# Output projections that begin with the upper features of three tiles, in the ring's banks

## What is computed

```
# first block, per layer
x = x + 0.5 * swiglu(rmsnorm(x), ...)
x = x + mixer(rmsnorm(x))          # layer 0: HGRN2, layer 1: forgetting attention (FoX)
x = x + 0.5 * swiglu(rmsnorm(x), ...)
# inside a mixer: o is (256, 1024), 8 or 16 heads side by side, times a gate
return o @ w_out                    # w_out is 1024 x 1024
# second block, per layer
mix = nsa_mixer(...)  or  mla_mixer(...)            # 12 heads of 64
xa = memory_cross_attention(xq, mk, mv)             # 4 heads of 64
y = concatenate([mix, xa], -1) @ w_out[i]
x = layer_norm(ALPHA * x + y);  x = layer_norm(ALPHA * x + hier_moe(x))
```

## Time and profile before

| | |
|---|---|
| runs of the kernel | 2225.61, 2226.37, 2236.63 us, median 2226.37 |
| profiled execution | 2233.53 us, of which its span is 2231.7 us |
| mean granted clock of TensorE | 0.978 |
| PE busy | 2108.8 us (94%), 14195 matmuls |
| DVE busy | 1483.2 us (66%) |
| ACT busy | 1157.1 us (52%) |
| POOL busy | 26.1 us (1%) |
| HBM read | 416.7 MB, 187 GB/s over the span |

### The profile page before, as it was taken

How to read it: one execution, slowest core, us unless ns; L and a number is a source line. 1 busy time by engine, 2 the same in 40 slices (tenths; PEclk the granted TensorE clock), 3 DMA queues, 4 the chain that set the end, 5 groups by cost and what they waited for, 6 DMA issues and landing times. The chain is left out here.

```text
span 2231.7 us, 36800 instructions
## 1 busy us (share of the span) xinstructions
PE 2108.8 (94%) x14195; PEld 1892.5 (85%) x14195; DVE 1483.2 (66%) x2248; ACT 1157.1 (52%) x1655; POOL 26.1 (1%) x34
## 2 busy tenths in 40 slices
PE   7999999999999999889999988999999989999997
PEld 6999897999999978779998977787778758778876
DVE  5665675665666644476564456789888466888896
ACT  4343533534444335464433336678776455777774
POOL 1000000000000020000000000000000000000000
PEclk9999999999999999999999979999999999999999
DMA  8555222654445523334454521599996514799991
GB/s 278 191 196 177 95 82 90 216 179 169 170 170 175 197 80 128 138 114 170 169 186 143 148 73 58 180 328 334 342 317 212 217 38 170 244 318 325 318 358 56
DMA packets 312310, 421.09 MB, mean 189 GB/s; under 512 B 7844, under 2 KB 266304, under 8 KB 312096
## 3 DMA queue, kind: packets, MB, share of 16 engines
q1 hardware_dynamic: 308864, 415.93, 54.5%
q10 hardware_dynamic: 2816, 2.38, 0.5%
q0 software_dynamic: 544, 1.62, 0.2%
HBM read 416.70 MB, written 1.05 MB: 187 GB/s over the span
## 5 line engine op out<-in xcount | busy, mean ns | idle before, releaser
L2816 DVE TENSOR_TENSOR w_lo<-weight_ring,w_hi 128x1024 fp32r<-128x1024 f32 x384 | 449.3, 1220 | 35.9 <-ACT w_hi L2665 31.2
L569 PE MATMUL banks<-x_hi,w_hi 128*128 128x256 f32 x1408 | 401.0, 285 | 8.5 <-DVE w_lo L522 7.7
L570 PE MATMUL banks<-x_lo,w_hi 128*128 128x256 f32 x1408 | 399.3, 284 | 0.0
L571 PE MATMUL banks<-x_hi,w_lo 128*128 128x256 f32 x1408 | 399.3, 284 | 0.0
L2665 ACT ACTIVATE w_hi<-weight_ring 128x1024 fp32r<-128x1024 f32 x384 | 382.3, 1053 | 21.4 <-PE banks L2552 21.3
L515 ACT ACTIVATE w_hi<-weight_ring 128x1024 fp32r<-128x1024 f32 x88 | 93.0, 1057 | 418.5 <-PE banks L571 418.3
L887 DVE TENSOR_TENSOR pieces<-weight_ring,pieces 128x512 fp32r<-128x512 f32 (+2 forms) x245 | 166.3, 689 | 193.8 <-ACT pieces L876 192.3
L876 ACT ACTIVATE pieces<-weight_ring 128x512 fp32r<-128x512 f32 (+2 forms) x245 | 150.9, 627 | 251.3 <-PE banks L823 244.5
L569 PEld LDWEIGHTS banks<-x_hi,w_hi 128*128 128x128 f32 x1408 | 271.2, 193 | 10.8 <-DVE w_lo L522 8.6
L570 PEld LDWEIGHTS banks<-x_lo,w_hi 128*128 128x128 f32 x1408 | 271.3, 193 | 0.1
L571 PEld LDWEIGHTS banks<-x_hi,w_lo 128*128 128x128 f32 x1408 | 271.2, 193 | 0.0
(11 more groups left out here) (367 smaller groups left out, 3907.3 us busy)
## 6 DMA issues: line engine op xcount, KB each, us to landing
weight_ring<-in_ffn_w_in SPq DMA_DIRECT2D x88, 1024.0 KB, 7.5
weight_ring<-in_moe_w_gate SPq DMA_DIRECT2D x64, 1024.0 KB, 6.6
weight_ring<-in_moe_w_up SPq DMA_DIRECT2D x64, 1024.0 KB, 9.2
weight_ring<-in_moe_w_down SPq DMA_DIRECT2D x64, 1024.0 KB, 11.1
weight_ring<-in_ffn_w_out SPq DMA_DIRECT2D x44, 1024.0 KB, 9.6
weight_ring<-in_hg_w_in SPq DMA_DIRECT2D x12, 1024.0 KB, 8.2
weight_ring<-in_fox_w_in SPq DMA_DIRECT2D x12, 1024.0 KB, 8.5
weight_ring<-in_nsa_w_in SPq DMA_DIRECT2D x10, 1024.0 KB, 7.8
```

The source lines that it names most:

```text
L569: pe.matmul(out, w_hi, m_hi, start=start, stop=False, skip_group_check=True)
L570: pe.matmul(out, w_hi, m_lo, start=False, stop=False, skip_group_check=True)
L571: return pe.matmul(out, w_lo, m_hi, start=False, stop=stop, skip_group_check=True)
L2816: dve.tensor_tensor(self.piece(s, p, self.w_lo), self.piece(s, p), self.piece(s, p, self.w_hi.bitcast(F32)), ALU.subtract).then_inc(sem[ki ...
```

## The change

The order of the pieces of w_out becomes (tile 0, upper half), (1, upper), (2, upper), (0, lower), (1, lower), (2, lower), and from tile 3 on tile by tile as before. The results go to four banks of the ring, two tiles each, in place of banks 0 to 3; DVE releases each bank once its residual is written. Low and high parts of `cat` are made by helpers of their own (`act_cat_hi`, `dve_cat_lo`), and in the attention stages three of each, and the first three pieces, move into the last steps of the loops. A quarter is collected ahead of the score of its step. The last pair is always copied by ACT. `pr` no longer uses `wide[:, 0]`, which now takes high parts during the attention; two of its pairs lie in a region that only Ffn and Moe use otherwise. In Hgrn2 the pieces and the first two low parts come between the second and the third quarter.

```diff
--- before.py
+++ after.py
...
+        with ExitStack() as split:
+            split.enter_context(nc.sbuf_tensor("before_units", [P, ARENA + 4 * KD * T], F32))
+            self.more_units = split.enter_context(nc.sbuf_tensor("more_units", [P, 2, 2, 2 * T], F32))
...
         self.act_pieces(act, self.in_pieces + PIECES)
-        for c in range(4):
-            act.wait_ge(self.cat_ready, c + 1)
-            act.activation(k.half[0][:, 2 * c:2 * c + 2], k.cat[:, 2 * c:2 * c + 2], ACT.Copy).then_inc(k.xs_hi, 1)
+        for c in range(self.act_cat, 4):
+            self.act_cat_hi(act, c)
         self.act_pieces(act, "out7")
 
+    def act_cat_hi(self, act, c):
+
+        k = self.k
+        act.wait_ge(self.cat_ready, c + 1)
+        act.activation(k.half[0][:, 2 * c:2 * c + 2], k.cat[:, 2 * c:2 * c + 2], ACT.Copy).then_inc(k.xs_hi, 1)
+        self.act_cat = c + 1
+
+    def dve_cat_lo(self, dve, c):
+
+        k, cs = self.k, slice(2 * c, 2 * c + 2)
+        dve.wait_ge(k.xs_hi, self.hi0 + 4 + c + 1)
+        dve.tensor_tensor(k.half[1][:, cs], k.cat[:, cs], k.half[0][:, cs].bitcast(F32), ALU.subtract).then_inc(k.xs_lo, 1)
+        self.dve_cat = c + 1
+
     def release(self, eng, fill):
 
...
     def plan_out(self, name, w_out):
         k = self.k
-        self.w_out, self.out_fills = w_out, [k.ring.plan(1), k.ring.plan(1)]
+        self.w_out, self.out_fills, self.out_name = w_out, [k.ring.plan(1), k.ring.plan(1)], name
+        self.act_cat = self.dve_cat = 0
...
+        k = self.k
         self.in_pieces = len(self.piece_list)
-        for n in range(KD):
+        self.out_order = [(n, half) for half in range(2) for n in range(PIECES)] + [(n, half) for n in range(PIECES, KD) for half in range(2)]
+        self.out_piece = {}
+        for n, half in self.out_order:
             fill = self.out_fills[n // 4]
-            w = self.k.ring.slot(fill)[:, 0:4096].rearrange("p (k n) -> p k n", k=KD)
-            self.jobs[f"out{n}"] = self.plan_pieces(fill, w, slice((n % 4) * P, (n % 4 + 1) * P), 4)
+            w = k.ring.slot(fill)[:, 0:4096].rearrange("p (k n) -> p k n", k=KD)
+            self.out_piece[n, half] = k.n_pieces
+            self.piece_list.append((k.n_pieces, fill, w[:, 4 * half:4 * half + 4, (n % 4) * P:(n % 4 + 1) * P]))
+            k.n_pieces += 1
             self.job_end[f"out{n}"] = len(self.piece_list)
+
+    def plan_out_banks(self):
+        for c in range(4):
+            self.k.banks.plan_by(f"{self.out_name}_o{c}", self.k.piece_used, PIECES + self.out_piece[2 * c + 1, 1] + 1)
...
     def pe_out(self, pe):
-        k = self.k
-        for n in range(KD):
-            self.pe_tile(pe, k.acc[:, n], self.jobs[f"out{n}"], P, (k.half[0], k.half[1]), None if n else self.cat_split)
+        k, b = self.k, self.k.banks
+        for n, half in self.out_order:
+            name, m = f"{self.out_name}_o{n // 2}", self.out_piece[n, half]
+            if n % 2 == 0 and half == 0:
+                b.claim(pe, name)
+            out = b.at(name)[:, n % 2 * T:(n % 2 + 1) * T]
+            hi, lo = self.piece_parts(m, 4, P)
+            pe.wait_ge(k.piece_lo, m + 1)
+            for j in range(4):
+                kk = 4 * half + j
+                if n == 0 and kk % 2 == 0:
+                    pe.wait_ge(k.xs_lo, 4 * self.cat_split + kk // 2 + 1)
+                last = self.pe_three(pe, out, (hi[:, j], lo[:, j]), (k.half[0][:, kk], k.half[1][:, kk]), n % 2 == 0 and kk == 0, kk == KD - 1)
+            last.then_inc(k.piece_used, 1)
 
     def dve_out(self, dve, scale=1.0):
 
         k = self.k
         self.dve_pieces(dve, self.in_pieces + PIECES)
+        for c in range(self.dve_cat, 4):
+            self.dve_cat_lo(dve, c)
         for c in range(4):
-            cs = slice(2 * c, 2 * c + 2)
-            dve.wait_ge(k.xs_hi, self.hi0 + 4 + c + 1)
-            dve.tensor_tensor(k.half[1][:, cs], k.cat[:, cs], k.half[0][:, cs].bitcast(F32), ALU.subtract).then_inc(k.xs_lo, 1)
-        for c in range(4):
-            cs = slice(2 * c, 2 * c + 2)
+            cs, name = slice(2 * c, 2 * c + 2), f"{self.out_name}_o{c}"
             self.dve_pieces(dve, f"out{min(2 * c + 3, KD - 1)}")
-            dve.wait_ge(k.piece_used, PIECES + self.jobs[f"out{2 * c + 1}"][-1] + 1)
-            dve.scalar_tensor_tensor(out=k.x[:, cs], in0=k.x[:, cs], scalar=scale, in1=k.acc[:, cs],
+            src = k.banks.wait(dve, name).rearrange("p (k t) -> p k t", k=2)
+            dve.scalar_tensor_tensor(out=k.x[:, cs], in0=k.x[:, cs], scalar=scale, in1=src,
                                      op0=ALU.mult, op1=ALU.add).then_inc(k.x_ready, 1)
+            for done in ([], [0], [1], [2, 3])[c]:
+                dve.wait_ge(k.x_ready, 4 * self.turn + done + 1)
+                k.banks.release(dve, f"{self.out_name}_o{done}")
...
         k.banks.plan("hg_n", *[f"hg_r{n}" for n in range(4)])
+        self.plan_out_banks()
...
             dve.tensor_tensor(k.cat[:, hs], self.og[:, hs], src, ALU.mult).then_inc(self.cat_ready, 1)
             dve.wait_ge(self.cat_ready, n + 1)
             b.release(dve, f"hg_r{n}")
+            if n == 1:
+                self.dve_pieces(dve, self.in_pieces + PIECES)
+                self.dve_cat_lo(dve, 0)
+                self.dve_cat_lo(dve, 1)
         self.dve_out(dve)
...
-        self.pr = [part(t)[:, r] for t in (at, flat(k.wide[:, 0])) for r in range(2)]
+        self.pr = [part(at)[:, r] for r in range(2)] + [k.more_units[:, r] for r in range(2)]
...
             k.banks.plan(f"{name}_s{i}_0", f"{name}_s{i}_1")
+        self.plan_out_banks()
...
     def copied_by_dve(self, j):
-        return j % 4 == 3
+        return j % 4 == 3 and j < len(self.pairs) - 1
...
             if 0 <= j < n and not self.copied_by_dve(j):
                 out, src = self.copy_in(act, j)
                 act.activation(out, src, ACT.Copy).then_inc(k.att_copied, 1)
+            if step >= n - 1:
+                self.act_drain(act, step - n + 1)
             if step < n:
                 c = (self.u0 + step) % 4
                 for half in range(2):
@@ -1371,8 +1417,12 @@
                         e = self.pr[step % self.DEEP][:, half, at:at + w]
                         act.activation(e, e, ACT.Exp, scale=-1.0, bias=k.att_cols[:, 0, c, t, half:half + 1],
                                        accum_out=k.att_cols[:, 1, c, t, half:half + 1]).then_inc(k.att_exp, 1)
-        act.wait_ge(k.att_turned, self.u0 + n)
-        self.act_pieces(act, self.in_pieces + PIECES)
+    def act_drain(self, act, at):
+
+        if at != 2:
+            self.act_cat_hi(act, (0, 1, None, 2)[at])
+        if at:
+            self.act_pieces(act, self.in_pieces + at)
 
     def dve_units(self, dve):
...
-            if step < n:
-                self.dve_score(dve, step)
-            if 1 <= step < n + 1:
-                self.dve_weight(dve, step - 1)
             if q < 4 and step - self.VALUE_LAG - 1 >= self.quarter_end[q]:
                 self.dve_quarter(dve, q)
                 q += 1
-        self.dve_pieces(dve, self.in_pieces + PIECES)
+            if step < n:
+                self.dve_score(dve, step)
+            else:
+                self.dve_cat_lo(dve, step - n)
+            if 1 <= step < n + 1:
+                self.dve_weight(dve, step - 1)
+            if step >= n:
+                self.dve_pieces(dve, self.in_pieces + step - n + 1)
         while q < 4:
             self.dve_quarter(dve, q)
             q += 1
```

## The result

The changed kernel took 2217.66 us (median of 14 runs, 2212.14 to 2223.54) beside 2231.98 us for the kernel before (14 runs, 2225.45 to 2236.63): a ratio of 0.9941, 95% interval 0.9930 to 0.9952, so 13.1 us less. The forecast was 13.0 us less, 2213.4 beside the 2226.37 of that time. A second measurement, at the end of the study, gave 2218.94 us and 0.9959 (0.9945 to 0.9973), 9 us less; the two intervals overlap from 0.9945 to 0.9952, 11 to 12 us less. The profiled execution took 2213.9 us, its span is 2212.0 (before: 2231.7).

What follows compares the result with a forecast made beforehand. PE was busy 2108.81 of 2231.70 us, so time could be won only where it idles or runs at the lower clock. Terms: 6.9 - 0.2 + 4.3 + 2.0 + 0.4 - 0.4 = 13.0 us less, 2213.4; range 2206 to 2222.

Steps and rivals of the forecast that it cites:

- Start of the projection: In FoX, NSA and MLA, PE's waits before the out projection go: 6.88 us gained, less 0.2 for FoX.
- Cover: In the FoX, NSA and MLA projections, the fourth piece is ready 0.6 us before PE wants it: no cost.
- Rival C: The projection runs dry at its fourth piece in three stages: only 4 to 8 us gained; chance 0.08.
- Clock behind the starts: In FoX, NSA and MLA, the first projection matmuls no longer run at the low clock: 4.3 us gained.
- Rival B: The clock falls all the same in the attention stages: only 8.7 us gained, 2217.7; chance 0.19.
- HGRN2's start: In HGRN2, the first low part comes earlier and PE starts the projection 2.03 us earlier.
- HGRN2's clock: In HGRN2's projection, the clock's return gains 0.4 us, taken between 0.8 worse and 1.2 better.
- The added waits: DVE's wait on its own last residual before releasing a bank delays both Ffn stages: 0.4 us lost.
- Quarters ahead of scores: In the attentions, collecting a quarter before a score gains nothing, within 0.3 us either way per attention.
- step 1: In FoX, NSA and MLA, the out projection starts without PE's wait: 6.88 us gained, less 0.2 for FoX.
- Rival E: Kernel slower: new half-clock stretches, up to 13.5 us each, two needed to be over 0.5% slower, 2240; chance 0.04.

Runs made afterwards that it cites:

- Tile order: The changed kernel with the pieces of w_out tile by tile again, all else as changed; mean 2220.2 us, ratio 0.9953 to the kernel before.
- HGRN2 back: The changed kernel with HGRN2's three pieces and first two low parts behind all four products again; mean 2221.9 us, ratio 0.9961 to the kernel before.

## Why the prediction was right

1. **Start of the projection: right in place, a little small.** From the first score to the first projection matmul FoX went from 30.70 us (941.47 to 972.17) to 28.01 (936.11 to 964.12), MLA from 32.79 to 30.15; NSA's wait of 2.65 is gone. That is 8.0 us, where 6.7 were counted. (In this trace NSA's attention begins with 0.9 us at half clock and the projection starts 41.15 us behind the first score, before 43.43; in six other traces with the early splits and full clock there it is 40.69 to 40.71, 2.7 less.) The forecast had FoX's value products 0.2 us later; from the first score to the end of the last they came 0.39 us earlier (28.47 to 28.08), in MLA 0.56. Most of that is not the splits' doing: without them it is 28.11 in FoX.
2. **Cover: right.** The fourth piece was ready at 967.71 in FoX; PE wanted it at 964.12 + 4.3 = 968.4, so the cover is 0.7 us (0.6 counted). Tile order shows what it is worth: 2.2 us without the first three pieces' order. Rival C fell.
3. **Clock behind the starts: right at the place.** All three stretches are gone. Rival B fell there. What the whole kernel gained by it is less sure: the mean clock gives 4.5 us over 24 runs, against 4.7 counted with HGRN2, but 2.7 on one chip. What was missing in the reasoning is that the clock is not a matter of this gap alone. Dummies that kept it up at the place won nothing in the time, twice. And 3.4 us at half clock come and go inside MLA's attention, in kernels with the early splits (31.65 us from first score to projection with them, 30.15 without) as in kernels with late ones; each costs 1.5 us, as much as the term for one stage.
4. **HGRN2's start: right in this pair, a little high.** From the first product into `cat` to PE's start 6.33 us (373.08 to 379.41) became 4.32 (371.61 to 375.93): 2.01 against 2.03. Of these, 1.69 are the new order (HGRN2 back) and 0.33 an earlier fall of the clock in the trace of before, which the forecast took for a fixed part of the stage.
5. **HGRN2's clock: near by luck.** 21 intervals in 4.56 us lose 4.56 - 21 x 0.12 = 2.04, against 2.66 before: 0.6 better, 0.4 counted. In the other traces with the same HGRN2 code 14 to 22 intervals are slow, in the other traces with the old order there 14, 22 and 28. So this term moves by itself by more than it was said to be worth, and a gain is not shown.
6. **The added waits: right.** 0.5 us more in the Ffns, 0.4 counted, and moving the release took 0.4 of it away. Behind the last residual, which starts at 401.20 in HGRN2, DVE's next operation starts at 402.03, 0.83 us later. The Trainium skill, VectorE: DVE Perf Modes, section The DRAIN you can't avoid, has a semaphore behind each operation free. It does not speak of an engine that waits for its own result, and for such a wait the trace shows 0.83 us where the kernel before has 0.60 (405.32 to 405.92).
7. **Quarters ahead of scores: a small miss.** Taken as nothing; by its own experiment 0.25 us in FoX, inside the bound of 0.3, and 0.46 in MLA, outside it. These 0.7 us are part of the 8.0 of step 1.

The rows at the places add up to 8.0 + 4.3 + 2.0 + 0.6 - 0.5 = 14.4 us; the runs say 13.1, then 9. Without the clock the rows say 9.5 (9.2 with HGRN2's start at 1.7) and the runs at equal clock 7.3 (error 0.4), or 8.2 (error 0.6) on one chip. The missing 1 to 2 us have no row that shows them: this stays open. The split by the mean clock also left 1.4 and 1.9 us without a row where dummies moved no start, so it may be the split that is off and not the rows. Rival E did not come: the long stretch of half clock in NSA's input products is in both traces. So the mechanism was right, and that the sum of 13.0 met the first measurement to a tenth was luck: the start was counted 1.3 us too low, the clock is not shown to have given back its whole term, and over both measurements the sum was some 1.2 us high.

## What to carry over

When PE waits at the seam between two stages for the last of several inputs that pass through other engines, order the new stage's work so that it begins with what depends on the early inputs only, and put these conversions into the queues ahead of the old stage's last steps; the start came 2.6 to 2.7 us earlier per stage, and the order behind it was worth 0.7 to 0.9 us per stage. Keep what the old stage still needs (here the copy of the last pair) off the engine that takes the extra work, and ahead of it. Filling an idle gap with dummies over 128 rows held the clock there, but count the time of the whole kernel before calling it won. Read what a wait costs from the starts of matmuls: the idle times before L824 in the tile order missed a third of it.

## What was not expected of the hardware

- Dummies of zeros over 128 rows held the granted clock at 1.00 behind the gap, and won no time: mean clock 0.9809 with them and 0.9802 without, where the stretches kept would have made 0.9823, and 0.9792 against 0.9816 where there was no gap to fill. Where the loss goes, and what decides it, is not shown.
- Dummies over 8 rows took the same time (2.11 us for 9) and did not hold it: 0.64 in the window behind. HGRN2 fits this: its clock falls in 372 to 374 (0.90 there, 0.50 in 374 to 376) while PE runs the products over 8 rows of L1151. That these are the cause is a reading; no run changed them.
- The time and the mean clock of a run move together, 2.05 us for 0.001. The changed kernel's own first 14 runs spread over 11 us, with clocks from 0.980 to 0.986, and of one trace only differences at the place can be trusted: this pair of traces differs by 19.7 us, the medians by 14.
